# A tuned fp32 transformer kernel: two 192-byte tiles change places in SBUF, and the tiles behind them move by 192 bytes

## What is computed

```python
def reference(x, mem, positions, ..., mem_2, norm_mix_g_2, ...):
    x = first_block(x, mem, positions, rel_bias, ...)      # DEPTH = 2 layers
    return second_block(x, mem_2, ...)                     # DEPTH_2 = 1 layer
```

## The kernel before

| tile | start, bytes | modulo 256 |
|---|---|---|
| raw | 16512 | 128 |
| w_hi, w_lo | 32896, 57472 | 128 |
| x_t | 82048 | 128 |
| neg_max | 90240 | 128 |
| act_hi, act_lo, mem_t, cst | 90432, 98624, 106816, 115008 | 64 |
| sumsq | 132448 | 96 |
| row_sum | 141952 | 128 |
| qk_dil, probs, p_t, q_t, k_t, o_hi, o_lo, kx_t, vx, h_hi, h_lo | 142400 and up | 64 |

## Time and profile before

### The profile page before, as it was taken

The page is one execution under the profiler, slowest core; times in us unless marked ns, Lnnn a source line. Parts: engine busy times, 40 slices in busy tenths (PEclk is TensorE's granted clock), DMA queues, the critical chain, the costliest instruction groups (busy, mean ns, idle before and its releaser), DMA issues.

```text
span 1257.4 us, 23273 instructions
## 1 busy us (share of the span) xinstructions
PE 1218.1 (97%) x10107; PEld 1189.0 (95%) x10107; DVE 831.6 (66%) x970; ACT 668.2 (53%) x967; POOL 46.1 (4%) x41
## 2 busy tenths in 40 slices
PE   5999999999999999999999999999999998999998
PEld 4999999989999999999898999999899997999998
DVE  5778449686664488864867766447778876676442
ACT  5466545466543356654655654335476754565332
POOL 3000000000000000000000000100200100000000
PEclk9999999999999999999999999999989999999999
DMA  7734544336656643454434765664541453466552
GB/s 241 225 113 144 171 147 158 108 125 212 207 188 199 189 135 106 135 170 167 139 100 136 225 201 178 219 213 134 156 145 60 140 163 101 128 209 201 193 182 95
DMA packets 195571, 202.89 MB, mean 161 GB/s; under 512 B 5716, under 2 KB 191847, under 8 KB 195471
## 3 DMA queue, kind: packets, MB, share of 16 engines
q1 hardware_dynamic: 192704, 194.82, 48.5%
q0 software_dynamic: 2464, 5.99, 1.6%
q10 hardware_dynamic: 303, 0.61, 0.2%
HBM read 200.33 MB, written 3.16 MB: 162 GB/s over the span
## 4 chain that ended last, share of the span: by engine, by line
PE 84%; DVE 7%; ACT 5%; issue 2%; DMA 2%; POOL 0%; DVEq 0%; ACTq 0%; POOLq 0%
PE bank L593 14%; PE bank L594 14%; PE bank L595 14%; PE bank L2471 7%; PE bank L2473 7%; PE bank L2469 7%; ACT w_hi L543 2%; DVE w_lo L553 2%; PE bank L2379 2%; PE bank L2363 2%; PE bank L657 2%; PE bank L658 1%; PE bank L659 1%; PE bank L636 1%; DMA raw<-in_w_in_dram 1%
## 5 line engine op out<-in xcount | busy, mean ns | idle before, releaser
L553 DVE TENSOR_TENSOR w_lo<-raw,w_hi 128x2048 fp32r<-128x2048 f32 (+7 forms) x210 | 424.6, 2031 | 259.5 <-ACT w_hi L543 259.2
L543 ACT ACTIVATE w_hi<-raw 128x2048 fp32r<-128x2048 f32 (+7 forms) x210 | 355.6, 1705 | 333.5 <-PE bank L2473 109.7
L593 PE MATMUL bank<-act_hi,w_hi 128*128 128x256 f32 (+1 forms) x1104 | 307.4, 278 | 2.8 <-DVE w_lo L553 1.4
L595 PE MATMUL bank<-act_hi,w_lo 128*128 128x256 f32 (+1 forms) x1104 | 305.5, 277 | 0.0
L594 PE MATMUL bank<-act_lo,w_hi 128*128 128x256 f32 (+1 forms) x1104 | 305.4, 277 | 0.0
L593 PEld LDWEIGHTS bank<-act_hi,w_hi 128*128 128x128 f32 (+1 forms) x1104 | 206.8, 187 | 4.9 <-issue 2.9
L595 PEld LDWEIGHTS bank<-act_hi,w_lo 128*128 128x128 f32 (+1 forms) x1104 | 206.9, 187 | 0.1
L594 PEld LDWEIGHTS bank<-act_lo,w_hi 128*128 128x128 f32 (+1 forms) x1104 | 206.6, 187 | 0.2
L2469 PE MATMUL bank<-h_hi,w_hi 128*128 128x256 f32 x736 | 203.3, 276 | 0.0
L2473 PE MATMUL bank<-h_hi,w_lo 128*128 128x256 f32 x736 | 203.2, 276 | 0.0
L2471 PE MATMUL bank<-h_lo,w_hi 128*128 128x256 f32 x736 | 203.1, 276 | 0.0
(11 more groups left out here) (412 smaller groups left out, 2170.4 us busy)
## 6 DMA issues: line engine op xcount, KB each, us to landing
raw<-in_w_up_dram SPq DMA_DIRECT2D x32, 1024.0 KB, 5.3
raw<-in_w_down_dram SPq DMA_DIRECT2D x32, 1024.0 KB, 5.2
raw<-in_w_ff_dram SPq DMA_DIRECT2D x32, 1024.0 KB, 5.3
raw<-in_w_in_dram SPq DMA_DIRECT2D x23, 1024.0 KB, 5.4
raw<-in_w_xk_dram SPq DMA_DIRECT2D x8, 1024.0 KB, 5.1
raw<-in_w_xv_dram SPq DMA_DIRECT2D x8, 1024.0 KB, 5.1
raw<-in_w_mix_out_dram SPq DMA_DIRECT2D x8, 1024.0 KB, 5.4
raw<-in_w_xq_dram SPq DMA_DIRECT2D x8, 1024.0 KB, 5.1
```

Source lines behind the costliest of these rows:

```text
L543: ins = act.activation(d, r, ACT.Copy)
L553: ins = dve.tensor_tensor(d, r, h.bitcast(F32), ALU.subtract)
L593: pe.matmul(o, stat_hi, mov_hi, start=first, stop=False)
L595: return pe.matmul(o, stat_lo, mov_hi, start=False, stop=last)
```

## The change

Two of the small tiles are allocated elsewhere. No instruction is added, removed or put in another place in any engine's order, and none changes its shape. Operands move.

```diff
         raw = sb("raw", [P, RAW, SLAB])
+        neg_max = sb("neg_max", [P, 48])
         w_hi = sb("w_hi", [P, RING, SLAB], F32R)
         w_lo = sb("w_lo", [P, RING, SLAB], F32R)
         x_t = sb("x_t", [P, KD, T])
-        neg_max = sb("neg_max", [P, 48])
+        row_sum = sb("row_sum", [P, 48])
         act_hi = sb("act_hi", [P, KD, T], F32R)
         act_lo = sb("act_lo", [P, KD, T], F32R)
...
         rstd_c = sb("rstd_c", [P, 2, T])
-        row_sum = sb("row_sum", [P, 48])
         row_inv = sb("row_inv", [P, 48])
```

## The result

| | before | after |
|---|---|---|
| median of 4 runs | 1260.6 us | 1279.57 us |
| lowest to highest | 1258.17 to 1261.92 | 1276.74 to 1281.12 |
| profiled execution, its span | 1259.2, 1257.4 us | 1276.7, 1274.9 us |

The ratio is 1.015 (95% interval 1.0129 to 1.0172): slower by 19 us. The forecast was 1264.5 us, range 1251 to 1273, with 0.32 for slower. The time lies outside the range, on the side of rival 1.

What follows compares the result with a forecast made beforehand. It took how often TensorE can start a matmul as the bound. (528 + 384) x 4.6 ns = 4.2 us on 1259.2 gave 1263.4, in medians' terms 1263.4 to 1265.9; it took 1264.5 us, range 1251 to 1273.

Steps and rivals of the forecast that it cites:

- rival 1: Distance 0 slow in itself for all h and close o: 13.0 us, 1272; far end 17 us, 1276; chance 0.17.
- terms 1 to 3: ScalarE, VectorE, GpSimd on moved tiles; DMA; and operations on neg_max and row_sum: each priced at 0.
- Term 4: Products of act against w, both directions: distances stay at -64 and +64, so 0.
- Term 5: o against w, distance -64 to 0: close stretches on fresh starts turn wide, 528 matmuls at 4.6 ns each.
- wide six tenths: Share of o matmuls judged already at the slower pace, about 118.0 ns, before the change; forecast to stay there.
- Term 6: h against w, distance -64 to 0: of 2,304 matmuls only the last 384 slow, at 4.6 ns each; others inherit.
- Rival 2: Faster: 64 the better place for a moving operand, or 0 a good distance; 1252.5, far end 1247.7 us; chance 0.25.
- Rival 3: act at place 0 is a bad place: some 3,000 matmuls turn wide, 13.8 us, 1273; chance 0.05.
- Rival 4: No dependence on addresses: pace drawn at each start, change only draws anew; 1258 to 1262.5 us; chance 0.16.

Runs made afterwards that it cites:

- the map: Kernel before plus groups of 24 matmuls of one w_hi slab against itself at distances 0 to 256 bytes; run once, only its trace used.
- x_neg_only: Kernel before with only neg_max moved in front of w_hi, row_sum staying, so every product is at distance 0; 1301.14 us, ratio 1.0321.
- the two halves: Kernel before with one move each: only neg_max in front of w_hi, 1301.14 us; only row_sum in front of act_hi, 1277.76 us.
- x_h_back: Changed kernel with 192 unused bytes in front of qk_dil, restoring the distances of before at other places; 1271.2 us, ratio 1.0079.

## Why the prediction was wrong

**The bound.** TensorE's pace of starts as the only thing that this edit can change, and VectorE, ScalarE and DMA at 0 (terms 1 to 3): right, with 831.6 us of VectorE in both profiles.

**Term 4**, `act` against `w` at unchanged distances: right. 277 and 282 ns stayed, at new places.

**Term 5**, `o`: right in direction, short in size. The close ones turned slower, but the "wide six tenths" didn't stay where they were: at distance 0 all 1,248 settle at 120 ns. The 48 of `w` moving that were booked among the 528, as inheriting, stayed close at 113.3. The term measured 4.6 us against 2.4 (528 x 4.6).

**Term 6**, `h`, is the step that failed: "the runs of 768, 768 and 384 begin without a gap behind close `act` products; I take it that they inherit the close pace, as at 185.59 us". They don't. At 350.56 us, three matmuls into the down projection, three take 0.36 us, and the pace stays at 120 ns. All 2,304 pay: 15.2 us were measured where 1.8 (384 x 4.6) was booked. Two things were wrong in this step. A pace passes on without a gap where the distance stays the same, but `o` to `w` at 185.59 us was a change of distance, as is `act` to `h` after the change, and those products of the earlier trace rows come out close behind an `o` at 120 ns too. And distance 0 has no close pace to inherit: none was seen in the map, in `o` and `h` after the change, or in all products of x_neg_only.

The price of distance 0 was wrong too. The six matmuls of `weights_first` were the witness for distance 0, with starts 117 to 119 ns apart there, and they hadn't settled. The 0.48 us for four that followed them belongs to `act` at -64 on its way to the close pace. That it comes to the 120 ns of `h` afterwards is chance: it was taken as the far end of rival 1 and was no measurement of distance 0. The forecast itself priced distance 0 at the 4.6 ns of another distance, where it is 6.6 (120.0 against 113.4).

The prediction's count of the products is rough: `w` moving has 864 matmuls and `o` 1,248, not 768 and 1,152, and all together are some 8,570, not 8,700. No term of the sum hangs on these.

**The rivals.** Rival 1 (distance 0 is slower in itself, inherited or not) came true, at its far end: (2,304 + 528) x 6.6 = 18.7 us with the 120 ns, where the text gave 13 and "more, 17 us". The 19.8 us measured for `h` and `o` are more because the wide part of `o` slowed too, from 117.8 to 120.0. Its test, the first 50 matmuls behind the start of `h`, decided it. Rival 2 had two parts. "64 is the better place for a moving operand" is refuted: `w` moving now stands at 64 and has 282 ns. A good distance other than -64 does exist, but it is 112 and not 0. Rival 3 (`act` at 0 a bad place) is refuted by the 277 ns. Rival 4 (no dependence) is refuted by the two halves, with ratios 1.032 and 1.015. Its draw is real all the same at -64: between the two profiles the `act` stretches at 193 and 205 us changed places, 117.8 and 113.4 ns before, 113.5 and 117.8 after.

**The rule weighed against it.** The Trainium skill's "SBUF — State Buffer" ("Who interferes with whom") calls TensorE's two read ports independent. By that rule the sum was 0. The measurement decides otherwise for the sum: with the same shapes and the same work, starts lie 113.3 to 123.3 ns apart according to where the two operands start relative to each other. Whether the two ports are what gets in the way, no run here shows.

What stays open is the mechanism. The runs show that the pace depends on both operands' places and that distances 0 and 256 agree; that would fit two reads which get in each other's way, but no run showed such a meeting. Nor was it tried why single points like 112 are close while 4 bytes beside it aren't.

A correction of the text ahead of the prediction: `weights_first` issues its six matmuls ahead of the third slab of an MLP, and in the first block four more ahead of the output projection's first half slab.

## What to carry to other kernels

Where TensorE starts matmuls back to back, each with a weight load of its own, read the distance between starts in each stretch; two values at one shape and clock can come from the operands' places in SBUF or, at one pair of places, from how the stretch was entered. Here a tile of 192 bytes allocated elsewhere cost 1.5 to 3%. Map it with groups of the kernel's own matmul, displaced in steps of 16 bytes, with many matmuls a group and several entries to each: here up to fourteen went by before a group settled, and a distance could have two paces. Judge a placement by all the pairs that it makes together: two moves that cost 42 and 18 us alone cost 19 together.

## What was not expected of the hardware

- fp32r matmuls of 128x128 by 128x256 at the 2.4 GHz level started every 113.3 ns at best in these runs, and every 120.0 ns when both operands start at the same place modulo 256. The other steps of 16 bytes in the first map lie between 116.7 and 120.0, single steps of 4 bytes between 115.5 (188) and 123.3 (4).
- The pace is a state that lasts. At -64 both 113.3 (kernel before) and 117.8 ns (x_h_back) were held over 1,437 matmuls without a break. Within one execution the same stage drew 117.8 in two MLPs and 113.3 in the third (x_h_back). That executions of one program differ by this draw (1260.6 to 1277.3 us there) is likely, but only one of them was profiled.
- A stretch keeps its pace across a change of tiles if the distance stays. If it changes, the new pace needn't be that of the stretch before: at +64, 24 matmuls ran at 113.3 ns behind a stretch at 120.0, and at 118.0 behind one at 113.3.
- A distance of 112 was close from every one of 14 ways in, with the stationary operand at 128, and at all eight stationary places that are multiples of 32 bytes; 16 bytes off, it ran at 120.0 seven times and at 118.3 once.
